# Feed-forward gate and up tiles as seven block products instead of eight, with weight sums made partly by accumulating transfers

## What is computed

```python
def swiglu(x, w_gate, w_up, w_down):
    return (jax.nn.silu(x @ w_gate) * (x @ w_up)) @ w_down

def reference(x, mem, ...):
    for l in range(DEPTH):
        x = layer_norm(ALPHA * x + 0.5 * swiglu(x, ffn_w_gate[l, 0], ffn_w_up[l, 0], ffn_w_down[l, 0]), ...)
        x = layer_norm(ALPHA * x + hybrid_mixer(x, ...), ...)
        x = layer_norm(ALPHA * x + memory_attention(x, ...), ...)
        x = layer_norm(ALPHA * x + 0.5 * swiglu(x, ffn_w_gate[l, 1], ffn_w_up[l, 1], ffn_w_down[l, 1]), ...)
    return x
```

## Time and profile before

| | us |
|---|---|
| median of 3 runs | 1156.59 |
| lowest and highest | 1156.32, 1157.65 |
| span of the profiled execution (first to last instruction) | 1155.4 |
| TensorE busy | 1146.6 (99%) |
| VectorE busy | 573.1 (50%) |
| ScalarE busy | 420.6 (36%) |
| GpSimd busy | 33.5 (3%) |

### The profile page before, as it was taken

How to read it: one execution, slowest core, us unless ns; L and a number is a source line. 1 busy time by engine, 2 the same in 40 slices (tenths; PEclk the granted TensorE clock), 3 DMA queues, 4 the chain that set the end, 5 groups by cost and what they waited for, 6 DMA issues and landing times.

```text
span 1155.4 us, 14689 instructions
## 1 busy us (share of the span) xinstructions
PE 1146.6 (99%) x5456; PEld 957.1 (83%) x5456; DVE 573.1 (50%) x932; ACT 420.6 (36%) x685; POOL 33.5 (3%) x50
## 2 busy tenths in 40 slices
PE   9999999999999999999999999999999999999997
PEld 8888888888888888888898888889888888888886
DVE  4533333353337589764884765467333333343325
ACT  4412212232324377643463554345122122143222
POOL 2000000000001011000000000000000000000000
PEclk9999999999999999999999999999999999999999
DMA  8632233233222222342253341233322322332201
GB/s 277 220 104 96 91 98 102 91 111 107 91 91 73 92 65 80 113 146 73 74 169 105 110 146 55 73 109 128 110 91 91 106 93 91 100 118 91 94 33 73
DMA packets 33564, 120.86 MB, mean 105 GB/s; under 512 B 3900, under 2 KB 3916, under 8 KB 33264
## 3 DMA queue, kind: packets, MB, share of 16 engines
q1 hardware_dynamic: 30528, 109.07, 28.7%
q0 software_dynamic: 2992, 11.19, 2.8%
HBM read 118.13 MB, written 2.11 MB: 104 GB/s over the span
## 4 chain that ended last, share of the span: by engine, by line
PE 99%; DVE 1%; issue 0%; ACT 0%; DVEq 0%
PE ps L449 31%; PE ps L451 31%; PE ps L450 31%; PE ps L466 1%; PE ps L697 1%; PE ps L676 1%; PE ps L764 1%; PE ps L748 1%; PE ps L669 0%; PE ps L668 0%; PE ps L603 0%; PE ps L860 0%; PE ps L488 0%; PE ps L621 0%; PE ps L620 0%
## 5 line engine op out<-in xcount | busy, mean ns | idle before, releaser
L1356 DVE TENSOR_TENSOR wlo<-raw,whi 128x1024 fp32r<-128x1024 f32 x196 | 240.4, 1231 | 371.6 <-ACT whi L926 370.7
L449 PE MATMUL ps<-xth,whi 128*128 128x512 f32 (+1 forms) x916 | 353.6, 386 | 0.0
L451 PE MATMUL ps<-xth,wlo 128*128 128x512 f32 (+1 forms) x916 | 351.6, 384 | 0.0
L450 PE MATMUL ps<-xtl,whi 128*128 128x512 f32 (+1 forms) x916 | 351.4, 384 | 0.0
L926 ACT ACTIVATE whi<-raw 128x1024 fp32r<-128x1024 f32 (+1 forms) x203 | 206.4, 1039 | 153.0 <-PE ps L451 141.7
L451 PEld LDWEIGHTS ps<-xth,wlo 128*128 128x128 f32 x916 | 172.1, 188 | 34.4
L450 PEld LDWEIGHTS ps<-xtl,whi 128*128 128x128 f32 x916 | 172.3, 188 | 32.9
L449 PEld LDWEIGHTS ps<-xth,whi 128*128 128x128 f32 x916 | 172.2, 188 | 32.9
L449 PE MATMUL ps<-whi,hhi 128*128 128x512 f32 x480 | 187.8, 391 | 0.0
L451 PE MATMUL ps<-whi,hlo 128*128 128x512 f32 x480 | 186.9, 389 | 0.0
L450 PE MATMUL ps<-wlo,hhi 128*128 128x512 f32 x480 | 186.8, 389 | 0.0
(11 more groups left out here) (189 smaller groups left out, 992.6 us busy)
## 6 DMA issues: line engine op xcount, KB each, us to landing
raw<-in_units SPq DMA_DIRECT2D x204, 512.0 KB, 3.3
gb<-in_ln_g POOLq DMA_DIRECT2D x4, 512.0 KB, 4.1
gb<-in_ln_b POOLq DMA_DIRECT2D x4, 512.0 KB, 5.3
xn<-in_x POOLq DMA_DIRECT2D x4, 512.0 KB, 12.1
wb<-in_bias_by_key POOLq DMA_DIRECT2D x8, 256.0 KB, 3.1
out<-xn SPq DMA_DIRECT2D x8, 256.0 KB, 2.1
gsp<-g_rows POOLq DMA_DIRECT2D x1, 1024.0 KB, 4.9
memn<-in_mem_cols POOLq DMA_DIRECT2D x1, 1024.0 KB, 5.5
```

The source lines that it names most:

```text
L449: mm(dst, lh, rh, start=start, stop=False)
L450: mm(dst, lh, rl, start=False, stop=False)
L451: return mm(dst, ll, rh, start=False, stop=stop)
L1356: v.tensor_tensor(wlo[c % SPL][:, :], raw[c % RAW][:, :], whi[c % SPL][:, :].bitcast(F32), ALU.subtract).then_inc(lo_done, 1)
```

## The change

Tiles 4 to 21 of both feed-forwards (`FAST0 = 4`) no longer make 2 x 8 x 3 = 48 matmuls of 512 columns. Gate and up of a tile are seen as two block rows, the 1024 inputs as two halves (low, high), and the sequence as two halves of 256 (near, far). That is a 2 x 2 by 2 x 2 block product, and seven block products in Winograd's arrangement give it, each with 4 blocks of 128 input rows: 7 x 4 x 3 = 84 matmuls of 256 columns (`fast_part`). TensorE takes them in the order P1, P5, P4 of the tile before, P6, P2, P3, P7.

Four sums of x are made once per feed-forward (`combine_x` on VectorE, with the copies on ScalarE) between tile 1 and tile 2; for the first feed-forward GpSimd loads a second copy of transposed x (`xraw`, 2 MB). Four sums of weights are needed for each tile, 128 x 512 each, in a buffer `tsum` of which there is one per feed-forward. The first two start as plain loads (gate low, up high) to which GpSimd adds up low by two accumulating transfers (`accum_op`), issued once the plain loads have landed (`pair_sums`). VectorE makes the other two (`sums`), each from the one before. All four are split into high and low like a unit: `fast_hi` on ScalarE, `lo_both`, `lo_sums` and `lo_last` on VectorE. The partial results are combined by five small ScalarE instructions (`seed_near`, `copy5`, `copy6`, `near_gate`, `far_gate`) and five VectorE ones (`up_near`, `up_far`, `silu_near`, `silu_far`, `fast_h`) per tile, all but `fast_h` of 256 columns.

The loops of `ffn_up` are written out. P4 of tile 21 stands inside `down`, after the first two row blocks of its first unit. GpSimd loads the gates' columns and the first norm vectors after the first feed-forward's sums, and the copies of the gates' columns move behind the down loop.

```diff
--- before.py
+++ after.py
...
+        def fast_banks(f):
+            return ((2, 3, 4), (5, 0, 1))[f % 2]
+        def fast_count(n, f):
+            return FAST * n + f - FAST0 + 1
...
-            load_gb(0)
             for b in range(NB):
                 pool.dma_start(xn[:, b, :], x[0, b * P:(b + 1) * P, :]).then_inc(x_in[b], 16)
+            def pair_sums(n):
+                for f in range(FAST0, FT):
+                    c, q, t = U_FFN[n] + 2 * f, fast_count(n, f), tsum[n]
+                    if f > FAST0:
+                        pool.wait_ge(sums_lo_done, 2 * q - 3)
+                        pool.wait_ge(sums_done, q - 1)
+                    pool.dma_start(t[:, 0, :], units[c][:, 0:512]).then_inc(base_in, 16)
+                    pool.dma_start(t[:, 1, :], units[c + 1][:, 512:]).then_inc(base_in, 16)
+                    pool.wait_ge(base_in, 32 * q)
+                    for j in range(2):
+                        pool.dma_start(t[:, j, :], units[c + 1][:, 0:512], accum_op=ALU.add).then_inc(pair_in, 16)
             pool.wait_ge(small_in, 16 * SMALL)
+            pair_sums(0)
+            pool.wait_ge(unit_used, U_F1 + 2 * FT)
+            nc.gpsimd.memset(wg[:, :, :].bitcast(F32), 0.0).then_inc(pool_ok, 1)
+            pool.dma_start(wg_raw[:, :, :], gate_cols).then_inc(gate_in, 16)
+            load_gb(0)
             pool.wait_ge(unit_used, U_VA)
             pool.wait_ge(pool_ok, 2)
...
             load_gb(2)
-            pool.wait_ge(ln_done, NB * 3)
+            pool.wait_ge(unit_used, U_F2)
+            pair_sums(1)
+            pool.wait_ge(unit_used, U_F2 + 2 * FT)
             load_gb(3)
...
-                tile(FT - 1)
+                if n == 1:
+                    pe.wait_ge(xraw_done, 2)
+                for f in range(2, FAST0):
+                    tile(f)
+                for f in range(FAST0, FT):
+                    fast_tile(n, f)
...
+            def fast_part(dst, wh, wl, xh, xl, start=False):
+                for k in range(KT // 2):
+                    c = slice(k * P, (k + 1) * P)
+                    mm(dst, wh[:, c], xh[:, k, :], start=start and k == 0, stop=False, skip_group_check=True)
+                    mm(dst, wh[:, c], xl[:, k, :], start=False, stop=False, skip_group_check=True)
+                    last = mm(dst, wl[:, c], xh[:, k, :], start=False, stop=k == KT // 2 - 1, skip_group_check=True)
+                return last
...
+            def part4(n, f):
+                pe.wait_ge(up_far_done, fast_count(n, f))
+                fast_part(ps[fast_banks(f)[0]][:, near], sth[n][f % 2][:, 3, :], stl[n][f % 2][:, 3, :],
+                          xth[3 * n][:, high, far], xtl[3 * n][:, high, far]).then_inc(unit_used, 1)
...
+            def fast_tile(n, f):
+                u, par, q = U_FFN[n] + 2 * f, f % 2, fast_count(n, f)
+                xh, xl = xth[3 * n], xtl[3 * n]
+                a, b, c = (ps[j][:, near] for j in fast_banks(f))
+                bh, bl, th, tl = sbh[n][par], sbl[n][par], sth[n][par], stl[n][par]
+                pe.wait_ge(h_done, FT * n + f - 1)
+                need(u)
+                fast_part(a, bh[:, 0:512], bl[:, 0:512], xh[:, low, near], xl[:, low, near], True)\
+                    .then_inc(p1_done, 1)
+                pe.wait_ge(sums_lo_done, 2 * q - 1)
+                if f == FAST0:
+                    pe.wait_ge(xc_done, 4 * n + 4)
+                fast_part(c, th[:, 0, :], tl[:, 0, :], x5[n][0], x5[n][1], True).then_inc(p5_done, 1)
+                if f > FAST0:
+                    part4(n, f - 1)
+                pe.wait_ge(sums_lo_done, 2 * q)
+                pe.wait_ge(p1_copied, q)
+                fast_part(a, th[:, 2, :], tl[:, 2, :], x6[n][0], x6[n][1]).then_inc(p6_done, 1)
+                fast_part(b, bh[:, 512:1024], bl[:, 512:1024], xh[:, high, near], xl[:, high, near])\
+                    .then_inc(p2_done, 1)
+                need(u + 1)
+                pe.wait_ge(p5_copied, q)
+                fast_part(c, seh[par], sel[par], x3[n][0], x3[n][1]).then_inc(p3_done, 1)
+                pe.wait_ge(p6_copied, q)
+                fast_part(a, th[:, 1, :], tl[:, 1, :], x7[n][0], x7[n][1]).then_inc(unit_used, 1)
...
-                    for k in range(SPL):
+                    for k, blocks in ((0, order[:2]), (1, order[:2]), (0, order[2:]), (1, order[2:])):
+                        need_both(n, k)
+                        for b in blocks:
+                            if k == 0:
+                                first(b)
+                            last = product(n, k, b, k == 0, False)
+                        if blocks[-1] == order[-1]:
+                            last.then_inc(unit_used, 1)
+                        elif k == 0:
+                            part4(n // 3, FT - 1)
+                    for k in range(2, SPL):
...
+            def fast_hi(n, f):
+                c, par, q = U_FFN[n] + 2 * f, f % 2, fast_count(n, f)
+                before = f - 2 >= FAST0
+                slots = U_FFN[n] + 2 * FAST0 + 3 * par - SPL + 1
+                def both():
+                    act.wait_ge(raw_in[c % RAW], 16 * (c // RAW + 1))
+                    act.wait_ge(p2_done, q - 2) if before else act.wait_ge(unit_used, slots)
+                    fn(sbh[n][par][:, :], raw[c % RAW][:, :], ACT.Copy).then_inc(hi_done, 1)
+                def sums(j):
+                    act.wait_ge(sums_done if j else pair_in, q if j else 32 * q)
+                    act.wait_ge(unit_used, c - 3 + j if before else slots + 1 + j)
+                    pair = slice(2 * j, 2 * j + 2)
+                    fn(sth[n][par][:, pair, :], tsum[n][:, pair, :], ACT.Copy).then_inc(sums_hi_done, 1)
+                def last():
+                    u = c + 1
+                    act.wait_ge(raw_in[u % RAW], 16 * (u // RAW + 1))
+                    if before:
+                        act.wait_ge(p3_done, q - 2)
+                    fn(seh[par][:, :], raw[u % RAW][:, 512:], ACT.Copy).then_inc(hi_done, 1)
+                return both, sums, last
...
+                both, sums, last = fast_hi(n, FAST0)
+                both()
+                sums(0)
+                sums(1)
+                last()
+                tile(3)
+                for f in range(FAST0, FT - 1):
+                    both, sums, last = fast_hi(n, f + 1)
+                    seed_near(n, f)
+                    both()
+                    copy5(n, f)
+                    sums(0)
+                    if f > FAST0:
+                        far_gate(n, f - 1)
+                    sums(1)
+                    copy6(n, f)
+                    last()
+                    near_gate(n, f)
+                f, ud = FT - 1, u0 + 2 * FT
+                seed_near(n, f)
+                act.wait_ge(p2_done, fast_count(n, f - 1))
+                split(ud)
+                copy5(n, f)
+                act.wait_ge(unit_used, ud - 3)
+                split(ud + 1)
+                far_gate(n, f - 1)
+                split(ud + 2)
+                copy6(n, f)
+                act.wait_ge(sums_lo_done, 2 * fast_count(n, f))
+                split_h(n, 0)
+                split_h(n, 1)
+                near_gate(n, f)
+                act.wait_ge(p2_done, fast_count(n, f))
+                split(ud + 3)
+                act.wait_ge(p5_done, fast_count(n, f))
+                split_h(n, 2)
+                far_gate(n, f)
...
+            def sums(n, f):
+                c, t = U_FFN[n] + 2 * f, tsum[n]
+                g, u = raw[c % RAW], raw[(c + 1) % RAW]
+                dve.wait_ge(pair_in, 32 * fast_count(n, f))
+                dve.wait_ge(raw_in[(c + 1) % RAW], 16 * ((c + 1) // RAW + 1))
+                if f > FAST0:
+                    dve.wait_ge(sums_lo_done, 2 * fast_count(n, f) - 2)
+                step.link(v.tensor_tensor(t[:, 2, :], t[:, 0, :], u[:, 512:], ALU.add))
+                dve.wait_ge(raw_in[c % RAW], 16 * (c // RAW + 1))
+                v.tensor_tensor(t[:, 3, :], t[:, 2, :], g[:, 512:], ALU.add).then_inc(sums_done, 1)
+            def lo_both(n, f):
+                c, par = U_FFN[n] + 2 * f, f % 2
+                dve.wait_ge(hi_done, c)
+                v.tensor_tensor(sbl[n][par][:, :], raw[c % RAW][:, :], sbh[n][par][:, :].bitcast(F32), ALU.subtract)\
+                    .then_inc(lo_done, 1)
+            def lo_sums(n, f, j):
+                pair = slice(2 * j, 2 * j + 2)
+                dve.wait_ge(sums_hi_done, 2 * fast_count(n, f) - 1 + j)
+                v.tensor_tensor(stl[n][f % 2][:, pair, :], tsum[n][:, pair, :], sth[n][f % 2][:, pair, :].bitcast(F32),
+                                ALU.subtract).then_inc(sums_lo_done, 1)
+            def lo_last(n, f):
+                u, par = U_FFN[n] + 2 * f + 1, f % 2
+                dve.wait_ge(hi_done, u)
+                v.tensor_tensor(sel[par][:, :], raw[u % RAW][:, 512:], seh[par][:, :].bitcast(F32), ALU.subtract)\
+                    .then_inc(lo_done, 1)
...
+            def up_far(n, f):
```

(69 more changed lines are left out.)

207 lines of the change are left out of this document (154 added, 53 removed).

## The result

| | before | after |
|---|---|---|
| median (4 runs each), us | 1156.64 | 1318.9 |
| lowest and highest, us | 1156.32, 1157.65 | 1316.47, 1322.55 |
| span of the profiled execution, us | 1155.4 | 1314.7 |
| time of the profiled execution, us | | 1316.47 |

The changed kernel is slower: the ratio is 1.140, with a 95% interval from 1.139 to 1.142. The sign and the mechanism were forecast. The size was not: 1232 us were forecast, and 1319 lies above the range.

What follows compares the result with a forecast made beforehand. The `tsum` loop, 3.8 + 5.6 + 3.8 = 13.2 us, was to bound each tile; 17 loops plus 9.1 gave 233.5 us against 195.8 per feed-forward, 75.4 more in all: 1232 us from 1156.6, eight in ten between 1152 and 1288.

Steps and rivals of the forecast that it cites:

- TensorE's price: Tiles 4 to 21: 10.88 us a tile before, 10.07 after, so TensorE's work falls 29.0 us in all.
- Weight loads: Rival: weight loads of 191 ns bound the 256-column matmuls, 16.0 us a tile, 1343 us in all; chance 0.01.
- The ring: Loop through `tsum`: plain transfers, GpSimd's wait, accumulating transfers, VectorE's wait, sums, low parts; 13.2 us, a tile's lower bound.
- VectorE's share: VectorE's two sums and two low parts within each tile's `tsum` loop: 0.69 + 0.69 + 1.23 + 1.23 = 3.8 us.
- L: Length of each tile's `tsum` loop: 3.8 + 5.6 + 3.8 = 13.2 us, from 11.1 to 14.7.
- the plain pair: GpSimd's two plain transfers into `tsum` per tile, with wake, issue and landing: 0.30 + 0.53 + 3.0 = 3.8 us.
- the adding pair: Two accumulating transfers into `tsum` per tile, handling twice the bytes: 5.6 us, between 3.5 and 7.1.
- A: Time of the two accumulating transfers per tile: 5.6 us taken, 3.5 from below, 7.1 from above.
- The start: Before tile 4: x's combination hidden, first low part ready 3.8 us before TensorE ends tile 3; no wait.
- What I cost at nothing: Items given no time, such as x's second copy in the crowded start; some 5 us if it delayed units.
- Accumulating much dearer than twice the bytes: Rival: accumulating transfers cost more or collide with raw loads, pair 7.1 us, loop 14.7, time 1283; chance 0.13.
- The round trip: Rival: the `tsum` transfers hide within TensorE's 10.07 us a tile, time 1128 us; hidden wholly or partly, chance 0.14.

Runs made afterwards that it cites:

- pair_once: Changed kernel with the four transfers made for tile 4 only, the other tiles using its first pair of sums again (sums partly wrong): 1128.9 us, ratio 0.976.
- dve_sums: Changed kernel with no transfers for sums, VectorE making all four weight sums from the loaded units: 1128.0 us, ratio 0.975.
- thin_units: Changed kernel with SyncE's unit loads cut from 512 KB to 64 KB from unit 6 on (output wrong): 1278.0 us, ratio 1.105.
- plain_pair: Changed kernel with the second pair of transfers copying in place of adding, two of four weight sums left out: 1253.5 us, ratio 1.083.
- half_pair: Changed kernel with all four transfers moving 256 of 512 columns from tile 5 on (sums partly wrong): 1223.2 us, ratio 1.058.

## Why the prediction was wrong

**TensorE's price: right.** 29.0 us were worked out from 226.6 and 119.9 ns; 28.0 and 28.9 us came where nothing else bound but waits of 2 to 3 us at tile 4 (pair_once, dve_sums). Weight loads did not bound the short matmuls.

**The ring: right in every link.** The links and the waits on both sides hold, and VectorE's share was 3.70 us, against 3.8. What failed is the size of L, 15.4 us in place of 13.2, and in it first of all the plain pair.

**The plain pair: the step that failed.** It was mis-sized, and left without bounds. 3.5 us and a wake of 0.3 were taken from a single 256 KB transfer; the pair took 5.1 and 0.3. By thin_units 1.1 us of the difference of 1.6 come from the unit load at its side; the other 0.5 is what a pair needs beyond a single transfer when hardly anything runs beside it. The text had put the unit load beside the adding pair, where it costs nothing by thin_units. The range failed here too: only A was given a low and a high value, so L could not come out above 14.7. In 34 rounds this term is 54 of the 84 us that the profiled span exceeds the forecast one (1314.7 against 1230.8).

**The adding pair: 5.6 taken, 6.2 measured**, within its bounds of 3.5 to 7.1, 22 us in 34 rounds. The doubled price of a byte was right (2.1). The difference of 0.6 is about what the two adding issues take more on GpSimd, 1.78 us in place of 1.06; that this is its cause is argued and not shown.

Together, by the sums' starts, L is 15.58 us over the 17 rounds of the first feed-forward and 15.16 over those of the second (first sums at 49.11 and 314.04, at 912.61 and 1170.40), so 17 x (2.38 + 1.96) = 74 of the 84 us.

**The start: mis-sized in the first feed-forward, right by luck in the second.** The first low part of tile 4's sums was to come at E - 3.8, E being TensorE's end of tile 3. In the first feed-forward E is 49.8 us, so it should have come at 46.0; it ended at 52.8, 6.8 us late, and TensorE waited 1.9 us at tile 4, which the prediction had listed as a sign of being wrong. Two things add up. The opening (tiles 0 and 1) ended at 28.0, and h of tile 1 not 2.8 us later but 7.9, since low parts of units stand ahead of and between its four multiplications; the combination of x and the multiplications of tile 2 thus ended 4.4 us late. The kernel before showed this already, with h of tile 1 at 35.56 us and the opening's end at 27.9 (the last 2 us of the earlier trace rows are tile 2's, at the same spacing); the first line is its VectorE queue, the other two are the changed kernel's:

```profile
34.87 0.69 DVE L1423 SCALAR_TENSOR_TENSOR h<-eg,ps 128x512 f32<-128x512 f32 x1
```

```profile
35.21 0.69 DVE L1747 SCALAR_TENSOR_TENSOR h<-eg,ps 128x512 f32<-128x512 f32 x1
...
49.11 0.69 DVE L1651 TENSOR_TENSOR tsum<-tsum,raw 128x512 f32<-128x512 f32 x1 [2.44 <-DMA tsum<-in_units]
```

Then VectorE waited another 2.44 us for the first pair of sums, which the crowded start had delayed; "What I cost at nothing" had the second copy of x there without loss. In the second feed-forward the low part ended 3.9 us before E, against 3.8, but two errors cancel: h of tile 1 came 1.0 us behind the opening and not 2.8, and the two more sums for x, which the text had put into the opening, stood behind it (2.5 us).

**The rest.** Behind the last low part TensorE needed 12.4 us to the start of `down` and not 11.5, twice 0.9. Another 1.3 us came in the attention part, 1.0 of it at one bias load that took 4.1 us where it had taken 3.0 before. With the 74 and the 6.8 this makes the 84 us.

**The rivals.** Accumulating much dearer than twice the bytes was the nearest, at 1283 and 0.13, yet not by its own mechanism: the adding pair is near the price of twice the bytes, and the ring grew more in the plain pair (1.6 us against 0.6). The round trip did not hide.

The signs: rounds 15.4 us apart (13 forecast); GpSimd's wait for the plain pair about 4 (3 forecast); TensorE's wait before P7 but not before P1; a gap at tile 4 (none forecast); and matmuls not always 0.12 us apart, since the granted clock was lower.

## What to carry to other kernels

When a transfer's destination is a single buffer, write the ring down: every step from the buffer's release to its next release, whatever the engines' shares say. Here all engines had room (the busiest beside TensorE at 8 of 10 us) and the ring alone cost 185 us against a second buffer and 191 against two more additions on VectorE. And give every link of such a sum a high value from a transfer in company, since a round trip measured alone is its low end.

## What the runs showed of the hardware

- Two adding transfers of 256 KB from HBM onto SBUF took 6.2 us from first issue to use, two plain ones in the same place 4.3; with 128 KB each the adding pair took 4.4. An adding byte took 2.1 times a plain one's time in the queues, with whole and with half rows (150 and 147 GB/s), though the number of packets stayed the same.
- GpSimd took 1.78 us to issue two adding transfers, 1.44 for one adding and one plain, and 1.06 for two plain.
- With a gap in each tile TensorE's granted clock was lower: in 60 to 300 us 0.84 with rounds of 15.6 us (the changed kernel), 0.94 with 13.5 (plain_pair), 0.96 with 12.8 (half_pair), and 0.99 and 1.00 in the kernels without gaps. In 920 to 1090 us the first three had 0.91, 0.91 and 0.98, so the length of the gap doesn't settle it. Behind a gap in the kernel with two buffers the 256-column matmuls stood 0.21 us apart, at the lower of the two levels (1.2 GHz), where they stood 0.12 apart at 2.4:

```profile
62.28 0.21 PE ps L615
62.49 0.21 PE ps L616
62.71 0.21 PE ps L614
```

- In the changed kernel this cost little by itself, as far as the chain shows it: the matmuls stretched into time in which TensorE would have waited.
